# One block of constants, x in halves, and another order of the opening, in a two-block transformer kernel

## The reference

```
mod = silu(c) @ ada_w + ada_b                   # 2048 x 12288, six sections of 2048 columns
sh1, sc1, g1, sh2, sc2, g2 = split(mod, 6)
h = rms_norm(x, mix_pre_g) * (1 + sc1) + sh1
q, k, v, a, g = split(h @ w_in, ...)            # w_in: 2048 x 5120
attn = attention(q, k, v)                       # 8 heads of 128
u = silu(layer_norm(causal_conv(a * sigmoid(g)))) # 31 taps
x = x + g1 * rms_norm(concat(attn, u) @ w_out, mix_post_g)
h = rms_norm(x, ffn_pre_g) * (1 + sc2) + sh2
x = x + g2 * rms_norm((silu(h @ w_gate) * (h @ w_up)) @ w_down, ffn_post_g)
```

## Time and profile before

| | |
|---|---|
| median of the timed runs | 2589.51 us |
| profiled execution | 2587.09 us |
| its span | 2585.4 us |
| mean granted clock of TensorE | 0.996 of full |
| TensorE (PE) busy | 2515.3 us (97%) |
| VectorE (DVE) busy | 1825.3 us (71%) |
| ScalarE (ACT) busy | 1292.6 us (50%) |
| GpSimd (POOL) busy | 170.8 us (7%) |
| HBM traffic | 239 GB/s over the span |

### The profile page before, as it was taken

One profiled execution on the slowest core, in us unless ns is written; L12 is line 12 of the kernel. 1 busy time (PEld: TensorE's weight loads), 2 busy tenths in 40 slices (PEclk: granted clock), 3 DMA queues, 4 the chain that ended last, 5 costly groups with the idle time before them and its releaser, 6 DMA issues.

```text
span 2585.4 us, 37987 instructions
## 1 busy us (share of the span) xinstructions
PE 2515.3 (97%) x13318; PEld 2085.2 (81%) x13318; DVE 1825.3 (71%) x2258; ACT 1292.6 (50%) x1852; POOL 170.8 (7%) x287
## 2 busy tenths in 40 slices
PE   6999989899999999999999999999999999999999
PEld 5777877787888888887788888887888888888887
DVE  3349888777998888988755565555688866667565
ACT  2349755634444444465534242425566555655454
POOL 0012100231210000000101010100000000000000
PEclk9999999999999999999999999999999999999999
DMA  8989578699987888797454545454478865656554
GB/s 350 388 330 372 197 273 298 195 327 337 306 295 248 284 264 286 271 315 277 152 190 155 187 155 187 155 187 139 155 269 289 269 188 185 186 168 206 195 193 165
DMA packets 219536, 619.58 MB, mean 240 GB/s; under 512 B 20740, under 2 KB 26020, under 8 KB 208672
## 3 DMA queue, kind: packets, MB, share of 16 engines
q1 hardware_dynamic: 205648, 554.76, 62.8%
q0 software_dynamic: 12816, 60.64, 6.6%
q10 hardware_dynamic: 960, 2.70, 0.3%
HBM read 612.25 MB, written 5.77 MB: 239 GB/s over the span
## 4 chain that ended last, share of the span: by engine, by line
PE 78%; DVE 8%; DMA 7%; issue 3%; ACT 3%; SPq 0%; DVEq 0%; ACTq 0%; POOL 0%; POOLq 0%
PE ps L2369 12%; PE ps L2309 11%; PE ps L2311 11%; PE ps L2310 11%; PE ps L2371 6%; PE ps L2742 5%; PE ps L2743 5%; PE ps L2744 5%; DVE w_lo L1434 2%; DMA raw<-in_w_down 2%; PE ps L2344 2%; PE ps L2346 2%; PE ps L2348 2%; DMA ada<-in_ada_w 2%; ACT w_hi L794 1%
## 5 line engine op out<-in xcount | busy, mean ns | idle before, releaser
L1434 DVE TENSOR_TENSOR w_lo<-raw,w_hi 128x1024 fp32r<-128x1024 f32 x762 | 928.4, 1226 | 497.8 <-ACT w_hi L794 496.3
L794 ACT ACTIVATE w_hi<-raw 128x1024 fp32r<-128x1024 f32 x762 | 803.5, 1058 | 896.4 <-PE ps L2311 375.5
L2369 PE MATMUL ps<-h_both,w_hi 128*128 128x512 f32 (+1 forms) x1392 | 485.3, 394 | 1.8 <-DVE h_both L1519 0.8
L2309 PE MATMUL ps<-w_hi,h_both 128*128 128x512 f32 x1152 | 461.7, 401 | 7.5 <-DVE h_both L1519 5.5
L2311 PE MATMUL ps<-w_hi,h_both 128*128 128x512 f32 x1152 | 449.6, 390 | 0.0
L2310 PE MATMUL ps<-w_lo,h_both 128*128 128x512 f32 x1152 | 449.1, 390 | 0.0
L2371 PE MATMUL ps<-h_both,w_lo 128*128 128x256 f32 (+1 forms) x1392 | 388.5, 279 | 0.0
L2369 PEld LDWEIGHTS ps<-h_both,w_hi 128*128 128x128 f32 x1392 | 261.0, 188 | 63.2 <-DVE h_both L1519 1.4
L1446 DVE SCALAR_TENSOR_TENSOR acc<-ada,cact,acc 128x1024 f32<-128x1024 f32 x224 | 290.4, 1296 | 4.6 <-DMA acc<-in_b_ada 1.9
L2742 PE MATMUL ps<-w_hi,f_hi 128*128 128x512 f32 x680 | 265.1, 390 | 1.2 <-DVE z_up L2185 0.8
L2309 PEld LDWEIGHTS ps<-w_hi,h_both 128*128 128x128 f32 x1152 | 216.5, 188 | 61.0 <-issue 7.4
(11 more groups left out here) (282 smaller groups left out, 3055.9 us busy)
## 6 DMA issues: line engine op xcount, KB each, us to landing
ada<-in_w_ada SPq DMA_DIRECT2D x192, 512.0 KB, 4.3
raw<-in_ffn_w_up SPq DMA_DIRECT2D x160, 512.0 KB, 4.4
raw<-in_na_w_qkv SPq DMA_DIRECT2D x96, 512.0 KB, 4.8
raw<-in_w_gate SPq DMA_DIRECT2D x88, 512.0 KB, 5.0
raw<-in_w_up SPq DMA_DIRECT2D x88, 512.0 KB, 4.9
raw<-in_w_down SPq DMA_DIRECT2D x88, 512.0 KB, 5.6
raw<-in_ffn_w_down SPq DMA_DIRECT2D x86, 512.0 KB, 4.5
raw<-in_w_in_tiles SPq DMA_DIRECT2D x80, 512.0 KB, 6.8
```

The costliest lines, as they stand in the source:

```text
L794: act.activation(w_hi[:, s, :], raw[:, s, :], ACT.Copy).then_inc(hi_ready, 1)
L1434: dve.tensor_tensor(w_lo[:, s, :], raw[:, s, :], w_hi[:, s, :].bitcast(F32), ALU.subtract).then_inc(lo_ready, 1)
L2309: pe.matmul(o, hi_[:, k, a], wh, start=(k == 0), stop=False)
L2369: pe.matmul(ps[:, 4 * part + g, :].rearrange("p (a n) -> p a n", a=2)[:, :, n], w_hi[:, s, a], h_both[:, :, k, n], start=(k == 0 and ts[-1 ...
```

## The change

- One array `constants` of 401 columns, laid out on the host, holds ident, ones, the vectors, bias_c and one column with 1 in rows 0, 32, 64 and 96 (`pick_1`). ScalarE's queue loads it in one DMA, in place of vecs and bias_c, and of what GpSimd made.
- x is loaded in two halves, rows 128 to 255 first, each with its semaphore.
- The seeds of the sums' banks are gone; VectorE clears both banks with a memset at the start. TensorE's waits for sel, pick_c and ada_rows stand behind the opening.
- Group 2 goes ahead of the last two pieces of transposes. ScalarE's first copy of sums no longer waits for all xn_t; before start_hi(0) it waits for two of them.
- The order of groups and tiles: tile 0, groups 4 and 5, tile 1, groups 6 and 7, tile 2 with the picks of eighth 1; then for e from 2: two groups, tile 3e-3, two groups, tile 3e-2 with the picks of e, tile 3e-1. `hi` and `lo` of the first tile of eighth 1 move behind start_hi(1) and start_lo(1). SP's queue gets groups 4 to 7 between tiles 0 to 3.
- GpSimd's wait for the eighth h_lo goes; groups 32 and 33 wait only for their slots (groups 28 and 29 done), and the two small loads come behind them. Group 34 still waits for the eighth h_lo.

The core of the diff:

```diff
+        consts = at("consts", [P, 401], S0)
+        ident, ones, vecs = consts[:, 0:128], consts[:, 128:256], consts[:, 256:368]
+        bias_c, pick_1 = consts[:, 368:400].rearrange("p (a k) -> p a k", a=2), consts[:, 400:401]
...
-            sp.dma_start(x[:, :, :], ins["x"][0].rearrange("(t p) d -> p t d", p=P)).then_inc(x_landed, 16)
+            for t in (1, 0):
+                sp.dma_start(x[:, t, :], ins["x"][0, t * P:(t + 1) * P, :]).then_inc(x_landed[t], 16)
...
             for n in range(3):
                 mixer_tile(n)
-            for e in range(1, EIGHTHS):
+                if n < 2:
+                    first_group(4 + n)
+            first_group(6)
+            first_group(7)
+            for n in range(3, 6):
+                mixer_tile(n)
+            for e in range(2, EIGHTHS):
...
-            pool.wait_ge(hlo_ready, EIGHTHS)
-            pool.dma_start(cvec[:, :], ins["conv_columns"]).then_inc(small_landed, 16)
-            pool.dma_start(fcw[:, :, :], ins["ffn_conv_columns"]).then_inc(small_landed, 16)
             for g in range(START_GROUPS, GROUPS):
                 group(g)
+                if g == START_GROUPS + 1:
+                    pool.dma_start(cvec[:, :], ins["conv_columns"]).then_inc(small_landed, 16)
+                    pool.dma_start(fcw[:, :, :], ins["ffn_conv_columns"]).then_inc(small_landed, 16)
...
-            act.dma_start(vecs[:, :], ins["vector_columns"]).then_inc(vec_landed, 16)
-            act.dma_start(bias_c[:, :, :], ins["first_bias_columns"]).then_inc(vec_landed, 16)
+            act.dma_start(consts[:, :], ins["constants"]).then_inc(consts_landed, 16)
...
-            act.wait_ge(xt_used, 8)
             for e in range(EIGHTHS):
-                if e:
+                if e >= 2:
                     hi(T_AG, 3 * e)
                 evacuate_sums(e)
+                if e == 0:
+                    act.wait_ge(xt_used, 2)
+                elif e % 2 == 0:
+                    act.wait_ge(xt_used, e + 2)
                 start_hi(e)
-                if e == 0:
-                    hi(T_AG, 0)
+                if e < 2:
+                    hi(T_AG, 3 * e)
...
+            dve.memset(ps[:, 6:8, :], 0.0).then_inc(banks_clear, 1)
+            dve.wait_ge(consts_landed, 16)
...
-                if g % 4 == 0 and e < 2:
-                    pe.matmul(ps[:, 6 + b, :], ident[:, :], ada_rows[:, :], start=True, stop=False)
...
             group(1)
+            group(2)
             x_columns(6, 8)
-            group(2)
             group(3)
             all_of(pick_columns(0))
             pe.wait_ge(rstd_read, 1)
-            for e in range(1, EIGHTHS):
+            start_tile(0)
+            group(4)
+            group(5)
+            start_tile(1)
+            group(6)
+            group(7)
+            start_tile(2, pick_columns(1, 10))
+            for e in range(2, EIGHTHS):
                 n, g = 3 * e - 3, 4 * e
-                start_tile(n)
                 group(g)
                 group(g + 1)
-                start_tile(n + 1)
+                start_tile(n)
                 group(g + 2)
                 group(g + 3)
-                start_tile(n + 2, pick_columns(e, 10))
+                start_tile(n + 1, pick_columns(e, 10))
+                start_tile(n + 2)
```

More of the change, by code:

```diff
@@ L163, in program @@
         S0 = 202 * KB
[L164 to L175, removed]
+        consts = at("consts", [P, 401], S0)
+        ident, ones, vecs = consts[:, 0:128], consts[:, 128:256], consts[:, 256:368]
+        bias_c, pick_1 = consts[:, 368:400].rearrange("p (a k) -> p a k", a=2), consts[:, 400:401]
+        cact = at("cact", [P, 48], S0 + 1632)
+        fcw = at("fcw", [P, 4, 86], S0 + 1824)
+        qg = at("qg", [P, HD], S0 + 3200)
+        kg = at("kg", [P, HD], S0 + 3712)
+        cols = at("cols", [P, 10, KD], S0 + 4224)
+        stat = at("stat", [P, 64], S0 + 4864)
+        eps_rms = at("eps_rms", [P, 1], S0 + 5120)
+        eps_ln = at("eps_ln", [P, 1], S0 + 5152)
         tab = at("tab", [DR * H2, LANES], S0 + 5184)
@@ L221, in program @@
         acc_bias = [sem(f"acc_bias{i}") for i in range(3)]
-        vec_landed = sem("vec_landed")
+        consts_landed = sem("consts_landed")
+        banks_clear = sem("banks_clear")
         small_landed = sem("small_landed")
-        x_landed = sem("x_landed")
+        x_landed = [sem(f"x_landed{t}") for t in range(NT)]
         ctx_landed = sem("ctx_landed")
@@ L619, in link @@
                 pool.wait_ge(pool_step, steps[0])
-            link(pool.memset(ident[:, :], 0.0))
             pool.memset(eps_rms[:, :], RMS_EPS)
             pool.memset(eps_ln[:, :], LN_EPS)
[L624 to L627, removed]
+            pool.memset(zero[:, :], 0.0).then_inc(const_ready, 1)
             pool.memset(mean1[:, :], 1.0 / (H1 * HD)).then_inc(const_ready, 1)
@@ L631, in _ @@
             pool.dma_start(ada_rows[4:28, :], ins["ada_b"].rearrange("a (r n) -> (a r) n", n=C)).then_inc(rows_landed, 16)
[L632 to L636, removed]
             link(pool.memset(pick_c[:, :, :], 0.0))
@@ L846, in ctx_modulated @@
                     s.then_inc(tr_free[b], 1)
-            act.activation(stat[:, 60:61], ones[:, 0:1], ACT.Silu)
-            act.wait_ge(vec_landed, 32)
+            act.activation(stat[:, 60:61], zero[:, :], ACT.Silu)
+            act.wait_ge(consts_landed, 16)
             act.activation(cact[:, :], vecs[:, 0:48], ACT.Silu).then_inc(cact_ready, 1)
@@ L1598, in _ @@
                 start_lo(e)
-                if e == 0:
-                    lo(T_AG, 0)
+                if e < 2:
+                    lo(T_AG, 3 * e)
                 lo(T_AG, 3 * e + 1)
@@ L1667, in _ @@
             off = [0]
[L1668 removed]
+            dve.wait_ge(const_ready, 5)
             dve.wait_ge(small_landed, 32)
@@ L2516, in _ @@
             con = (hc_hi, hc_lo)
-            pe.wait_ge(const_ready, 2)
+            pe.wait_ge(consts_landed, 16)
             def group(g):
@@ L2535, in group @@
                                    slots[slot][:, r // 2, r % 2 * EC:(r % 2 + 1) * EC],
-                                   start=(e >= 2 and g % 4 == 0 and r < 4), stop=(sec == 1 and half == 1 and r >= 4))
+                                   start=(g % 4 == 0 and r < 4), stop=(sec == 1 and half == 1 and r >= 4))
                 mm.then_inc(group_done, 1)
@@ L2545, in pick_columns @@
                 for o in range(4):
-                    mm = pe.matmul(ps[:, 6 + b, o:o + 1], sums[:, o * P:(o + 1) * P], pick[:, 28:29], start=True, stop=True)
+                    mm = pe.matmul(ps[:, 6 + b, o:o + 1], sums[:, o * P:(o + 1) * P], pick_1[:, :], start=True, stop=True)
                     if o == 3:
@@ L2586, in x_columns @@
                     e, t = n // 2, 1 - n % 2
+                    if n < 2:
+                        pe.wait_ge(x_landed[t], 16)
                     if n >= 6:
@@ L3000, in _ @@
                        [(1, (K - 1) // RING, None), (-(-(K + 1) // RING), (2 * K - RING) // RING, None)], RING)
-_INS = ["x", "ada_w", "ada_first", "ada_b", "vector_columns", "first_bias_columns", "conv_columns", "ffn_conv_columns",
+_INS = ["x", "ada_w", "ada_first", "ada_b", "constants", "conv_columns", "ffn_conv_columns",
         "mix_post_g", "w_in_tiles", "w_out", "ffn_post_g", "w_gate", "w_up", "w_down", "ctx_2",
@@ L3025 @@
     laid = {"ada_first": np.ascontiguousarray(first.transpose(4, 3, 0, 2, 1, 5)).reshape(32, P, 4, C),
-            "vector_columns": np.ascontiguousarray(columns("c", "c_2", "c_ctx_2", "mix_pre_g", "ffn_pre_g", "norm_mix_g_2",
-                                                           "norm_ffn_g_2")),
-            "first_bias_columns": np.ascontiguousarray(np.asarray(inputs["ada_b"])[0, :2 * D].reshape(2, KD, P).transpose(2, 0, 1)),
+            "constants": np.ascontiguousarray(np.concatenate([
+                np.eye(P, dtype=np.float32), np.ones((P, P), np.float32),
+                columns("c", "c_2", "c_ctx_2", "mix_pre_g", "ffn_pre_g", "norm_mix_g_2", "norm_ffn_g_2"),
+                np.asarray(inputs["ada_b"])[0, :2 * D].reshape(2 * KD, P).T,
+                (np.arange(P) % 32 == 0).astype(np.float32)[:, None]], axis=1)),
             "conv_columns": np.ascontiguousarray(np.concatenate([columns("conv_b", "conv_ln_g", "conv_ln_b"), conv_w], axis=1)),
```

17 lines of the change are left out of this document (7 added, 10 removed).

## The result

The changed kernel takes 2572.22 us (2571.44 to 2572.61) against 2589.25 us in the same comparison: ratio 0.9934, 95% interval 0.9917 to 0.9951. Run twice more on other occasions it gave 2574.22 us (0.9946, 0.9931 to 0.9960) and 2572.81 us (0.9948, 0.9932 to 0.9963). It is faster, by 14.5 to 17.0 us between the medians. The forecast was 12.4 us.

What follows compares the result with a forecast made beforehand. TensorE was taken as the bound (busy 2515.3 of 2585.4 us), DMA nearly as full in the opening's rounds. Gains 5.7 + 0.9 + 6.8 - 1 - 1 + 1 = 12.4 us gave 2577 us, range 2571 to 2583.

Steps and rivals of the forecast that it cites:

- GpSimd's queue: Groups 32 and 33 loaded sooner, near 114 us: costs 0 to 5.1, taken 1; later slot waits give back 1.
- The start: Opening up to the first tile: sums copied at 21.4 instead of 27.10, first tile at 27.2; 5.7 us gained.
- The upper bound for the constants, 9.0: Opening loads: the block of constants lands by 9.0 us at the latest, still ahead of x's second half.
- The rounds: Opening's rounds: picks in the second of three tiles remove six 1.13 us waits for h_both, 6.8 us gained.
- the seed: First round: the second seed of the sums, 1.02 us at 38.01, goes; 0.9 us gained.
- the first boundary: Round boundary at e = 1: a 4.3 us chain, picks right ahead; about 1 us still waited, as now.
- The term for DMA: Loads in the rounds: DMA costs 0 to 3 us (418 to 400 GB/s), taken as 1.
- a clock below 1.00 behind 45 us: TensorE's granted clock after the first 45 us: a fall below full would show the prediction wrong.
- DMA did not bound the rounds: Rival, DMA bounds the rounds: 14.4 us a round at 400 GB/s, 7.5 us gained, 2582; chance 0.17.
- the case that the gain is hidden: Rival, rounds: engines hold only 364 GB/s, 15.8 us a round, 1.3 us gained, 2588; chance 0.06.
- More: Rival, opening: no DMA loss, 2.2 us of later waits gone, first tile at 2.4 GHz; 17.6 gained, 2572; chance 0.17.
- the slower case: Rival, rounds: SP's queue stands at tile loads, engines run empty, TensorE drops to 1.2 GHz; 2598 at 17.5 us rounds; chance 0.03.

Runs made afterwards that it cites:

- GpSimd's old wait: Changed kernel with GpSimd's wait for the eighth h_lo put back ahead of its loads; 2573.17 us (0.9938), again 2572.80 us (0.9951).
- the third: Changed kernel with GpSimd's wait for the eighth h_lo put back and 15 unused TensorE products at the prob wait near 367 us; 2572.07 us (0.9938).

## Why the prediction was right, and where it wasn't

The time, 2572.2 us for a forecast of 2577, lies near the low end of its range. At w_lo 40 the lead is 12.5, 13.6 and 13.1 us in three profiles, for a forecast of 12.4. That the first is within 0.1 us is luck: start and rounds gained 1.8 us more than forecast, and GpSimd's queue lost 1.7 that weren't. What came behind w_lo 40 (15.7 us between the first spans, 17.0 between the first medians) wasn't forecast at all.

- **The start: 5.7 forecast, 6.4, 6.3 and 6.7 measured.** The steps hold one by one: x at 9.6, group 3 after its landing, the copy at once, the chain of 5.9 us behind it unchanged. Group 3 was done at 20.6 and not 21.3. The upper bound for the constants, 9.0, was 2.1 us too high, and nothing hung on it. That the copy no longer waits for all xn_t brought 0.7 us, and x in halves nothing.
- **The rounds: 0.9 for the seed, 6.8 and less 1 for DMA, so 6.7 forecast; 7.8, 8.2 and 8.1 measured** from the first tile to the end of tile 23. Tile 21 starts at 125.9 to 126.5, not at 128. The waits for h_both went at six boundaries, as worked out. In the first profile the sum closes: 6.8 us for the six, 0.6 at the first boundary, which was counted as unchanged (0.50 us is left of 1.13), 0.8 to 1.0 for the seed, less 0.6 us of new waits for groups, make 7.6 to 7.8. The term for DMA was no mistake. Those waits were 0 to 2.0 us in the eleven profiles with the new order, 1.1 in the mean, while the engines moved 416 to 417 GB/s at a share of 1.02.
- **GpSimd's queue: the step that failed.** The text reads "That costs 0 to 5.1 us; I take 1, since most of group 31 is through by then" and takes 1 us back later: nothing in sum. Measured against the kernel before, the stretch from the end of tile 23 to w_lo 40 lost 1.7, 0.9 and 1.6 us. With GpSimd's old wait it gained 1.5 us in two profiles and nothing in the third. At w_lo 40 that is 2.5 to 3.7 us between the changed kernel and the first two (16.1 and 16.2), and none against the third (13.0). The size is inside the bounds given. The place isn't: group 31 was indeed through; the raw tiles 24 to 26 were late, through them the sigmoid, and TensorE waited 2.8 to 3.1 us and then ran at the lower clock. I had followed only who waits for the next groups, and not who stands behind the tiles in SP's queue and behind the roundings in ScalarE's. In the timed runs this cost doesn't show; what makes up for it is open.
- **The clock.** One of the prediction's own signs of being wrong, a clock below 1.00 behind 45 us, came: 0.58 over 140 to 145 us. The sum had no term for it. For all that follows the opening it allowed 1.5 us either way; up to 2.7 us was measured at one place. Up to 360 us the lead of the first profile moved between 11.5 and 13.4 and stood at 12.7 at the end. Behind that the leads of three profiles of the changed kernel end at 12.3, 14.6 and 15.7.
- **The rivals.** DMA did not bound the rounds. They took 13.75 to 13.78 us at 417 GB/s, on a core alone, so the case that the gain is hidden had no ground. That is above the HBM limit of about 358 GB/s that the Trainium skill gives (DMA: Bandwidth & Descriptors, Specifications), and the trace decides here. "More" came near in its number, without its means: the first tile still ran partly at 1.2 GHz (clock 0.50 over 25 to 30 us). Nothing showed the slower case; the longest wait for a group in the rounds was 0.64 us in the first profile of the changed kernel, 1.16 in the other two, and 1.63 in the variants.

## What to carry to other kernels

When a transfer is issued sooner, follow every transfer that it may pass, down to the last consumer, and not just the next one: here 2.1 MB, the first half of which was needed 30 us later, delayed three tiles, a rounding queue and a sigmoid. The same head start gave 2.2 us by w_lo 40 in the kernel before, whose engines had room, and cost there once another part of the same change had filled them. Neither could be seen in timed runs, so such an effect is to be read in more than one profile. Moving a short chain of engine hops so that one more tile of matmuls covers it was worth the whole gap, at six boundaries.

## What the runs showed of the hardware that wasn't expected

At the same wait of TensorE, 2.75 to 2.79 us long at some 370 us, the granted clock fell (to 0.56 to 0.81 of full in the worst 5 us) in seven of thirteen profiles and held in six, with one and the same kernel on either side. Each fall cost 1.3 to 2.7 us of 2570. At tile 24 there was no such mixture: the clock fell in all five profiles that waited 2.82 to 3.17 us there, for 1.2 to 2.4 us more up to the wait for u_pad, and held in all nine that waited 1.27 to 1.83 us. A difference of that size between single profiles of this kernel, and a "gain" in code that a change doesn't touch, is to be looked up in the clock's column first.
